# Two transformer blocks on one core: how GpSimd splits the weights, which engine masks the gate, and where the PSUM bank counter starts

## The reference, cut to what matters

```python
for l in range(DEPTH):                       # first block, DEPTH = 2
    h = rmsnorm(x, attn_norm[l])
    (q, kc, vc, ksl, vsl, kwn, vwn, gts, gq, gk, gv, ga, gr, uv) = split_columns(h @ w_in[l])
    o_nsa = nsa_mixer(q, kc, vc, ksl, vsl, kwn, vwn, gts, ...)   # gates = sigmoid(gts)
    o_gla = gla_mixer(gq, gk, gv, ga, gr, ...)
    o_sg = spatial_gating(uv, ...)
    x = x + concat([o_nsa, o_gla, o_sg]) @ w_out[l]
    h = rmsnorm(x, ffn_norm[l])
    x = x + (silu(h @ w_gate[l]) * (h @ w_up[l])) @ w_down[l]
x = rmsnorm(x, final_norm)                   # then the second block:
proj = h @ w_in_2                            # xa, za, q, k, v, zb, ga, gb; h = modulated norm of x
merged = sigmoid(ga) * (y_a @ w_pa) + sigmoid(gb) * (y_b @ w_pb)
x = x + gate * (merged @ w_o)
```

## Time and profile before

| | us |
|---|---|
| median of 3 runs (2049.79 to 2055.84) | 2050.62 |
| the profiled execution, its own time | 2054.61 |
| its span | 2052.6 |
| TensorE busy | 1924.2 |
| GpSimd busy | 1419.6 |
| VectorE busy | 1160.2 |
| ScalarE busy | 615.6 |

### The profile page before, as it was taken

One profiled execution on the slowest core, in us unless ns is written; L12 is line 12 of the kernel. 1 busy time (PEld: TensorE's weight loads), 2 busy tenths in 40 slices (PEclk: granted clock), 3 DMA queues, 4 the chain that ended last, 5 costly groups with the idle time before them and its releaser, 6 DMA issues.

```text
span 2052.6 us, 28491 instructions
## 1 busy us (share of the span) xinstructions
PE 1924.2 (94%) x10022; PEld 1489.2 (73%) x10022; DVE 1160.2 (57%) x1670; ACT 615.6 (30%) x1116; POOL 1419.6 (69%) x1208
## 2 busy tenths in 40 slices
PE   7898889999999999988899999997999999989997
PEld 5676557888888877755588888885777777768775
DVE  5765774466257347478556704654937666650353
ACT  4124662210011131266531100113036566540111
POOL 8554117988789985511298978886897878757772
PEclk9999989999999999999999999998999999999998
DMA  5132002343334222300124433542132233222221
GB/s 204 53 96 80 22 11 83 122 143 108 97 121 136 92 72 81 116 21 22 32 93 123 133 100 96 148 124 67 51 108 84 79 94 87 76 72 93 84 91 41
DMA packets 68680, 182.44 MB, mean 89 GB/s; under 512 B 23888, under 2 KB 24144, under 8 KB 68432
## 3 DMA queue, kind: packets, MB, share of 16 engines
q1 hardware_dynamic: 60480, 154.48, 24.8%
q10 hardware_dynamic: 8080, 26.32, 4.1%
HBM read 178.67 MB, written 2.10 MB: 88 GB/s over the span
## 4 chain that ended last, share of the span: by engine, by line
PE 70%; DVE 13%; ACT 7%; issue 6%; POOL 2%; DMA 1%; ACTq 0%; DVEq 0%; POOLq 0%
PE PS L402 21%; PE PS L406 20%; PE PS L405 20%; POOL w_lo L2083 2%; PE PS L691 1%; PE PS L653 1%; PE PS L641 1%; PE PS L441 1%; ACT P L1251 1%; ACT rg L1322 1%; DVE gN L1472 1%; DVE P L1946 1%; PE PS L538 1%; POOL w_hi L2079 1%; DVE PS L1620 1%
## 5 line engine op out<-in xcount | busy, mean ns | idle before, releaser
L2079 POOL TENSOR_TENSOR w_hi<-raw,const 128x256 fp32r<-128x256 f32 (+1 forms) x602 | 641.9, 1088 | 586.1 <-PE PS L402 578.2
L2083 POOL TENSOR_TENSOR w_lo<-raw,w_hi 128x256 fp32r<-128x256 f32 (+1 forms) x602 | 783.9, 1324 | 13.4
L402 PE MATMUL PS<-a_hi,w_hi 128*128 128x512 f32 x1616 | 651.7, 403 | 42.3 <-POOL w_lo L2083 14.1
L405 PE MATMUL PS<-a_lo,w_hi 128*128 128x512 f32 x1616 | 635.8, 393 | 0.0
L406 PE MATMUL PS<-a_hi,w_lo 128*128 128x512 f32 x1616 | 635.3, 393 | 0.0
L402 PEld LDWEIGHTS PS<-a_hi,w_hi 128*128 128x128 f32 x1616 | 307.1, 190 | 128.6 <-issue 46.0
L406 PEld LDWEIGHTS PS<-a_hi,w_lo 128*128 128x128 f32 x1616 | 307.2, 190 | 65.9
L405 PEld LDWEIGHTS PS<-a_lo,w_hi 128*128 128x128 f32 x1616 | 307.6, 190 | 64.8 <-issue 3.4
L1793 DVE TENSOR_TENSOR work<-PS,rstd 128x512 f32<-128x512 f32 x88 | 60.8, 691 | 147.6 <-PE PS L406 140.9
L402 PE MATMUL PS<-f_hi,w_hi 128*128 128x512 f32 x352 | 138.7, 394 | 0.0
L406 PE MATMUL PS<-f_hi,w_lo 128*128 128x512 f32 x352 | 138.0, 392 | 0.0
(11 more groups left out here) (290 smaller groups left out, 2494.1 us busy)
## 6 DMA issues: line engine op xcount, KB each, us to landing
raw<-weights SPq DMA_DIRECT2D x278, 512.0 KB, 3.5
work<-mod_w ACTq DMA_DIRECT2D x24, 512.0 KB, 3.6
work<-cmp_w ACTq DMA_DIRECT2D x8, 1024.0 KB, 5.6
bias<-rpb SPq DMA_DIRECT2D x256, 12.0 KB
rgw<-rgw ACTq DMA_DIRECT2D x8, 256.0 KB, 2.6
out<-xc SPq DMA_DIRECT2D x8, 256.0 KB, 2.0
const<-const SPq DMA_DIRECT2D x1, 1436.5 KB, 15.3
x<-x_t SPq DMA_DIRECT2D x4, 256.0 KB, 6.8
```

The source lines that it names most:

```text
L402: ins = nc.tensor.matmul(out, wh, hi, start=start, stop=False)
L405: nc.tensor.matmul(out, wh, lo, start=False, stop=False)
L2079: G.tensor_tensor(w_hi[:, r, k, :], raw[:, r, k, :], ones[:, k, :], ALU.mult).then_inc(pool_chain, 1)
L2083: ins = G.tensor_tensor(w_lo[:, r, k, :], raw[:, r, k, :], w_hi[:, r, k, :].bitcast(F32), ALU.subtract)
```

## The change

- GpSimd writes w_hi with `tensor_scalar` by the constant 1.0 and no longer reads the column of ones. The pieces are w_hi and w_lo in turn: one w_hi of 512 elements, then its w_lo (one of 512, or two of 256 in "fine" slots), then the second half. After every piece but a slot's last GpSimd waits for its own semaphore before it issues the next. Fine slots are those of `in`, the first two `out` slots of a layer, and `in2` below 48, other than slot 0. The loops are written out: all 278 slots in line.
- ScalarE multiplies the columns of `gN` by `rowok` with an activation, behind the sigmoid and a wait for it, and `emptied((l, "gate", "T"))` is raised by that second one. VectorE no longer has this operation.
- `pool_of["next"]` is set to 0 at the start of each layer.

```diff
@@ tensor
-                pool_of["banks"] = 4
+                pool_of["banks"], pool_of["next"] = 4, 0
@@ scalar
                     elif name == "gate":
                         act.wait_ge(*filling((l, name, "T")))
                         A(gN[:, :, :], PS[:, uses[(l, name, "T")][0], 0:NT * 24].rearrange("p (n c) -> p n c", c=24), ACT.Sigmoid)\
+                            .then_inc(act_chain.sem, 1)
+                        act.wait_ge(act_chain.sem, act_chain.raised())
+                        if l == 0:
+                            act.wait_ge(const_in, 16)
+                        A(gN[:, 0, 2:24:3], gN[:, 0, 2:24:3], ACT.Copy, scale=c_("rowok"))\
                             .then_inc(emptied((l, name, "T")), 1)
@@ vector
-
-                        g = gN[:, 0, 2:24:3]
-                        TS(g, g, c_("rowok"), None, ALU.mult).then_inc(dve_chain.sem, 1)
-                        dve.wait_ge(dve_chain.sem, dve_chain.raised())
@@ gpsimd
-                each = 8 // pieces
-                for n in range(pieces):
-                    k = slice(n * each, (n + 1) * each)
-                    G.tensor_tensor(w_hi[:, r, k, :], raw[:, r, k, :], ones[:, k, :], ALU.mult).then_inc(pool_chain, 1)
-                for n in range(pieces):
-                    k = slice(n * each, (n + 1) * each)
-                    pool.wait_ge(pool_chain, chain + n + 1)
-                    ins = G.tensor_tensor(w_lo[:, r, k, :], raw[:, r, k, :], w_hi[:, r, k, :].bitcast(F32), ALU.subtract)
+                each, per = 8 // hi_parts, lo_parts // hi_parts
+                for h in range(hi_parts):
+                    k = slice(h * each, (h + 1) * each)
+                    G.tensor_scalar(w_hi[:, r, k, :], raw[:, r, k, :], 1.0, None, ALU.mult).then_inc(pool_chain, 1)
+                    spent[0] += 1
+                    pool.wait_ge(pool_chain, spent[0])
+                    for q in range(h * per, (h + 1) * per):
+                        k = slice(q * 8 // lo_parts, (q + 1) * 8 // lo_parts)
+                        ins = G.tensor_tensor(w_lo[:, r, k, :], raw[:, r, k, :], w_hi[:, r, k, :].bitcast(F32), ALU.subtract)
+                        if q < lo_parts - 1:
+                            ins.then_inc(pool_chain, 1)
+                            spent[0] += 1
+                            pool.wait_ge(pool_chain, spent[0])
                 ins.then_inc(split_done, 1)
...
+            def fine_slot(n):
+
+                item = PLAN[n]
+                return item[0] == "in" or item[0] == "out" and item[2] < 2 or item[0] == "in2" and item[1] < 6 * KT
 
             pool.wait_ge(head_in, 16)
...
+            for n in range(SLOTS):
+                if n and fine_slot(n):
+                    split(n, 2, 4)
                 else:
...
+                    split(n, 2, 2)
```

More of the change, by code:

```diff
@@ L102 @@
              + [(m, k) for m in range(OUT_EARLY, KT) for k in range(KT)])
[L105 to L112, removed]
 def stream_plan():
@@ L2067, in _ @@
             G = nc.gpsimd
[L2069 to L2075, removed]
-                each = 8 // pieces
-                for n in range(pieces):
-                    k = slice(n * each, (n + 1) * each)
-                    G.tensor_tensor(w_hi[:, r, k, :], raw[:, r, k, :], ones[:, k, :], ALU.mult).then_inc(pool_chain, 1)
-                for n in range(pieces):
-                    k = slice(n * each, (n + 1) * each)
-                    pool.wait_ge(pool_chain, chain + n + 1)
-                    ins = G.tensor_tensor(w_lo[:, r, k, :], raw[:, r, k, :], w_hi[:, r, k, :].bitcast(F32), ALU.subtract)
+            spent = [0]
@@ new lines, in split @@
+            def split(n, hi_parts, lo_parts):
+                r = n % RING
+                pool.wait_ge(raw_in[r], 16 * (n // RING + 1))
+                if n >= RING:
+                    pool.wait_ge(slot_used, n - RING + 1)
+                each, per = 8 // hi_parts, lo_parts // hi_parts
[11 more added lines that the diff above has]
+                            pool.wait_ge(pool_chain, spent[0])
@@ L2084, in split @@
                 ins.then_inc(split_done, 1)
-            def pieces_of(turn):
-                return PIECES if any(beside_vector(item) for item in PLAN[turn * RING:(turn + 1) * RING]) else 1
+            def fine_slot(n):
+                item = PLAN[n]
+                return item[0] == "in" or item[0] == "out" and item[2] < 2 or item[0] == "in2" and item[1] < 6 * KT
             pool.wait_ge(head_in, 16)
[L2091 to L2103, removed]
-                else:
[L2105 to L2109, removed]
```

## The result

| | before | after |
|---|---|---|
| median, us | 2052.77 (4 runs, 2049.79 to 2055.84) | 2078.93 (4 runs, 2076.73 to 2084.73) |
| ratio, 95% interval | 1 | 1.0132 [1.0104, 1.0160] |
| profiled execution, its own time / span | 2054.61 / 2052.6 | 2079.89 / 2077.0 |
| TensorE / GpSimd busy | 1924.2 / 1419.6 | 1941.1 / 1649.9 |
| VectorE / ScalarE busy | 1160.2 / 615.6 | 1001.6 / 616.2 |

A forecast was written before the change was run, and what follows sets the result against it. TensorE was taken as the bound, busy 1924.2 of 2052.6 us. Mask -11.9 and +0.3, bank -7.5, GpSimd's operations +1 and +0.5, pauses -2.6 and -4 sum to -24.2, giving 2026 us; range 2010 to 2040.

The forecast's parts named there:

- The step that failed: GpSimd's w_hi of 512 elements priced at 1.02 us, bounds 0.5 to 1.5; nothing lost where TensorE is full.
- GpSimd becomes the bound: Rival: slow w_hi makes GpSimd set the pace where TensorE is full; 2091 us at w = 1.5, chance 0.05.
- the sum: All forecast terms over the whole kernel added together: -24.2 us.
- a fast w_hi: Rival: w_hi at 0.5 us shortens both slots by 1 us and VectorE's waits; 2021 us, chance 0.12.
- Mask, layer 0: Sigmoid to first crossed block, layer 0: moving the blocked mask to ScalarE gains 11.9 us, bounds 8.8 and 11.9.
- given back: Rival: pauses bring nothing, VectorE's decay steps wait instead; only mask and bank gain, 2038.5 us, chance 0.22.
- Bank counter: Start of layer 1: reset gives gk bank 1, removing TensorE's wait for gate's eviction; -7.5 us, bounds -5.1 and -7.5.
- Pauses: Second block and stage ends: a pause after every piece lets VectorE in; -2.6 us and, with halved pieces, -4.
- Pair 0 to 1: Second block: pauses shorten pair 0's blocked first P scaling; -2.6 us, bounds 0 and -2.9.
- the start of the second block: Where VectorE interleaves with GpSimd, longer GpSimd slots cost +1 us.
- the ends of the stages: Where TensorE waits for VectorE beside 1024-element pieces, halved pieces halve the remaining wait; -4 us, bounds 0 and -10.8.
- Loops: Writing out GpSimd's loops in line costs 0 us for fetching.

The follow-up runs named there:

- experiment 5: Changed kernel with each coarse slot's w_hi and w_lo one whole piece again; 2027.38 us, ratio 0.9880.
- experiment 1: Changed kernel with w_hi again the two-operand product with the column of ones; 2041.62 us, ratio 0.9944.
- experiment 4: Changed kernel with w_hi written by GpSimd's tensor_copy instead of tensor_scalar; 2017.54 us, ratio 0.9825.
- experiment 3: Kernel before with only the mask moved to ScalarE and the bank counter reset, GpSimd untouched; 2048.34 us, ratio 0.9972.
- experiment 7: Changed kernel with the two-operand product for w_hi and the mask back on VectorE; 2039.93 us, ratio 0.9939.
- experiment 9: Kernel before with GpSimd's loops written out and one wait on its own semaphore per slot; 2039.96 us, ratio 0.9932.
- experiment 2: Kernel before with w_hi by tensor_scalar, loops written out, pieces and order as before, no pauses; 2027.34 us, ratio 0.9878.
- 6: Changed kernel with the two-operand product for w_hi and no pauses, both w_hi halves issued first; 2035.48 us, ratio 0.9914.
- 10: Kernel before with w_hi by a copy, loops written out, pieces as before, no pauses; 2024.15 us, ratio 0.9847.
- experiment 12: Changed kernel with a copy for w_hi and every slot fine, pauses kept; 2016.10 us, ratio 0.9811.
- experiment 8: Kernel before with only GpSimd's loops written out in line; 2054.42 us, ratio 1.0009.

## Why the prediction was wrong

**The step that failed** is the price of GpSimd's new operation: "For w_hi of 512 I bound 0.5 (half, one operand of two gone) to 1.5 (half as much again), and take 1.02, the nearest row." It measured 1.49, at the far bound. From it followed "A coarse slot then takes 2 x 1.02 + 2 x 1.27 + 4 x 0.08 = 4.9 us" and "nothing in the stretches where TensorE is full". The slot takes 5.78 us, and 0.41 and 0.37 us more than TensorE needs in the mean of the 66 slots of each feed-forward part (26.9 and 24.6 us against experiment 5, over 66). The formula was right: the slower rival's slot at w = 1.5 is 5.86 (2w + 2.9, with four gaps; the trace has three, and none between slots: 5.78). Experiment 1 puts the operation back and experiment 5 the whole slot, and each alone frees the feed-forward parts. This rival, "GpSimd becomes the bound", got a chance of 0.05, with the argument that a one-operand product "a third slower than the two-operand one" was needed. It was slower by 43% (1.49 against 1.04), so a price inside my own bounds of 0.5 to 1.5 was enough for it, and 0.05 was too little.

**Luck in the rest.** The other parts gained 26.3 us where the sum had 24.2, but not as the sum had it. With w_hi at the price that the sum took (experiment 1) the same parts gain 13.9 us. The other 12 come with `tensor_scalar` itself, an effect that the sum did not have.

**The rival's size.** It had 2091, from 180 slots. Only the 132 of the feed-forward and the eight of wo pay (50.7 and 2.5 us). Beside `pa`/`pb` GpSimd needs 5.78 us too, but the gated products there keep their spacing of 11.0 us for two slots: the slots split ahead cover it. From 1864.73 us on GpSimd works there without a break. It has the slot of the third product ready 21.7 us before VectorE takes that product out, the slot of the thirteenth only 13.6 us before. At the first step of wo it is 12.1 us, and from the third step on TensorE goes at GpSimd's 5.79 us.

**The estimate from a page.** The forecast gave an estimate of w_hi at 0.55 us from the Trainium skill, GPSIMD Engine Reference, "Engine selection" (one-input operations roughly line-rate). The copy of experiment 4 agrees with it, at 0.61 us; `tensor_scalar` with 1.49 us does not, and the measurement decides. The rival "a fast w_hi", 2021, is what experiment 4 ran: 2017.5. Near in time, but it gave the fast w_hi some 5 us, and against experiment 1 it brought 24.

**Mask, layer 0: right in size, wrong in cause.** -11.9 was forecast and -12.2 measured. But the move of the mask brings none of it: alone it is given back (experiment 3, 42.96 us), and with the mask back on VectorE it stays (experiment 7). What brings it is whatever lets VectorE in beside GpSimd: one break per slot (experiment 9), `tensor_scalar` pieces without any break (2) or, as I read the traces, a shorter slot that catches up with TensorE (6, 10). The rival "given back" named this mechanism and bound it to pauses that bring nothing. It came in experiment 3. In the changed kernel it did not, and without the pauses (6) it did not come either.

**Bank counter: right in its stretch.** -7.5 forecast, and -7.8 in experiments 1, 3, 4 and 5; -6.2 in the changed kernel, where TensorE then waits for GpSimd, 1.1 us in two waits ("GpSimd does not hold it up", the forecast said). In experiment 3 some of it is lost later.

**Pauses: the sum near, the cause wrong.** Pair 0 to 1 gained 2.7 (2.6 forecast), but the start of the second block lost 2.7 (1 forecast): from the statistics to pair 1 the kernel takes 150.9 us after and 151.0 before, so the shorter P brought nothing. Of the ends of the stages only the one before wo gained, 9.1 us, where I had 4 for all: the waits of the earlier trace rows at L2038 and L2019 are gone. The pauses did not do it. Experiment 2 has neither pauses nor halved pieces and gains 8.1 us there, the product with halved pieces gains 5.6 with pauses (experiment 1) and 6.2 without (6), and one break per slot gains 1.2 (9). The attention stages neither gain nor lose by the change in a way that shows: over all kernels they take 280 to 286 us each, mostly longer where the granted clock is lower (0.95 against 0.98 in the two layers of experiment 1, 286.4 and 282.5 us; in experiment 12 it is not so, 285.7 us at 0.95 and 282.6 at 0.94). That (3.8 us more over both layers than before), and 4.0 us in pairs 1 to 7, of which leaving the pauses out gives back 2, are most of the 11 us by which the profiled execution of experiment 1 (-13.1) stays behind the forecast sum of -24.2.

**Loops: right**, nothing (experiment 8, ratio 1.0009).

**What stays open.** Why `tensor_scalar` of GpSimd takes 1.49 us where a copy takes 0.61, and why it lets VectorE in where the two-operand pieces and the copies did not at the mask. What makes a run of GpSimd shut VectorE out, since neither one piece nor the length of the run explains it. What exactly shortens the end before wo. The bank reset was not run by itself.

## What to carry to other kernels

Price an operation that no row shows at both its bounds, look at what the far one does where the bottleneck has no slack, and give that case the chance that the bound has: here 0.4 us per slot in 132 slots cost twice all the gains. Better still, time the operation first. Where one engine's run shuts another out, moving the blocked operation can leave the next one blocked (experiment 3); break the run that blocks it. One wait on its own semaphore per slot was enough here. For a cast on GpSimd, the copy was the fastest of the three forms tried.

## What the runs showed of the hardware that I had not expected

- GpSimd on 128x512 fp32 to fp32r: copy 0.61 us, product with a broadcast operand 1.04, subtraction of two full operands 1.29, `tensor_scalar` by a constant 1.49: of the two one-operand forms one is the fastest and one the slowest of the four.
- VectorE's mask took 19.83 us beside a gapless run of GpSimd (experiment 8), and 0.54 us when it came 0.7 us after a break of 0.08 us, inside a run of eight pieces without a pause (experiment 9). Neither one piece's time nor the run's length explains that by itself: 40 us into another gapless run VectorE's operations took 1.05 us each.
- A slower operation made the kernel before faster by 25 us (experiment 2), and VectorE's mask took 2.71 us beside it, with no break in GpSimd's run.
